# Decays of a chunked state-space scan: fp32r products of 32 rows and a mask product in place of triangles spread by GpSimd

## The chip, the core and the metric

The kernel runs on one core of a Trainium2 chip. A core has five engines that run side by side: TensorE (PE in the profile; its weight loads are the row PEld), VectorE (DVE), ScalarE (ACT), GpSimd (POOL) and SyncE (SP), which here only issues DMAs. The metric is device time in microseconds (us), as the median of several runs; lower is better.

## The reference, cut to what matters

The model is a block of dense layers (gated convolution, attention, cross attention, MLP), then a second block: a mixer that holds a Mamba-2 scan (SSD), and a product-key expert layer. The change is in the scan. With 256 tokens and 16 meta tokens the scan has three chunks of 128 positions (the first one only its last 16), 24 heads of 64 in 4 groups of 6 heads, and a state of 128:

```
a = dt * A                                   # per position and head
a_cs = cumsum(a)                             # inside a chunk
decay_in = exp(segsum(a))                    # segsum[i, j] = a_cs[i] - a_cs[j] for i >= j, else -inf
cb = einsum('bclgn,bcsgn->bgcls', Cc, Bc)
y_diag = einsum('bgcls,bgrcls,bcsgrp->bclgrp', cb, decay_in, x_dt)
```

For each of the 24 heads and two chunks a 128x128 matrix of decays is needed: the exponential of a difference of running sums, and zero above the diagonal. The rest of the scan (states of the chunks, their decay, the output from the state) is not changed.

## The kernel before

Products of the dense layers are made in fp32r pairs: each 512 KB block of weights is fetched by SP into one of four slots (`raw`), cast by ACT to its high part `wh`, and DVE subtracts to get the low part `wl`; PE then takes three products for each piece (`wh` by high and low rows, `wl` by high rows). A block may be fetched into a slot when the block four before it has been split, and cast when PE has used the one four before it. All engines follow an order written out by hand, with semaphores between them, so the sequence on each engine is that of the code.

Stages around the change, in order: the MLP of the first block; `post(2)` and `norm(4)` (residual and RMS norm, where PE has nothing else to do than keep its clock up); the `xbc` blocks in five groups of four, of which PE makes a product of 272 tokens each, ACT copies it from the bank `AO` to `XB`, and DVE runs a convolution of 16 instructions a group (`conv4`) and splits the next blocks; in between, `dtz` (the steps dt and the decays a) is made by DVE and ACT, and five small products of `dtz` with the triangles `upper`, `later` and `ones` give the running sums, of which ACT makes `exs`; then the `z` blocks with transposes; then the scan.

The scan is a loop of 16 steps k on PE, ACT and DVE: step k is three heads of a group (two steps a group, 8 steps a chunk). On PE step k is: `seg(k+1)`, which makes the three 128x128 matrices of differences of the next step in `AO`; the products of step k with `XDT` into `Y` (they wait for `seg_m`); a product with the state (`from_state`) in even steps, `second_state` in odd steps of the first chunk; and in nine steps the 24 products of an `sc` block (`sc_wide`), which is dense work of the next part laid in between. ACT takes the exponential of `AO` (`EE`), DVE multiplies it with the masked correlations `CBM` (`MM`). Before the change `seg` is

```
mm(AO[:, 0, 0:3 * P], later[:, :], AU[:, k % 2, :, :], True, True)
```

in plain f32, where `AU` (128 x 3 x 128) is the triangle `upper` times a head's decays, made on GpSimd by `decay_inputs(k)`, two steps ahead of PE. GpSimd also adds the skip term and multiplies with the gate for four pieces of the output (`skip_and_gate`), the places of three of them being set by `SKIP_AT`.

Of the kernel before, what the change touches and what calls it, by code (L numbers as in the profile page):

```python
# [23 lines left out]
P = 128  # L24
# [8 lines left out]
D = 1024  # L33
# [79 lines left out]
SKIP_AT = {7: (0, 0), 10: (0, 1), 11: (0, 2)}  # L113
# [3 lines left out]
WARM_UP, KEEP_WARM = 32, 32  # L117

# [22 lines left out]
def build(nc, stream, gain_cols, cols, rows, post_gains, x, mem, meta, keys_in, out, h2_spill):  # L141
    ctx = ExitStack()
    with ctx:
# [18 lines left out]
        ident = sb("ident", [P, P])  # L162
# [7 lines left out]
        stat = sb("stat", [P, 48])  # L170
        choice_at = (nc.sbuf_base + 31) // 32 * 32
# [6 lines left out]
        def at(name, shape, offset, dt=F32, base=None):  # L178
# [49 lines left out]
        AU = at("AU", [P, 2, 3, P], 124192)  # L228
# [65 lines left out]
        meta_ss, meta_rstd, meta_scaled = sem("meta_ss"), sem("meta_rstd"), sem("meta_scaled")  # L294
# [4 lines left out]
        v_out, f_prod, mv_out = sem("v_out"), sem("f_prod"), sem("mv_out")  # L299
# [19 lines left out]
        au_done, seg_prod, seg_exp, seg_m, y_prod = (sem(n) for n in (  # L319
            "au_done", "seg_prod", "seg_exp", "seg_m", "y_prod"))  # L320
# [8 lines left out]
        numbered, hot, g_prod, g_out = sem("numbered"), sem("hot"), sem("g_prod"), sem("g_out")  # L329
        hot2, ranked, curve, up_part = sem("hot2"), sem("ranked"), sem("curve"), sem("up_part")  # L330
# [98 lines left out]
        def _(sp):  # L429
# [49 lines left out]
        def _(act):  # L479
# [60 lines left out]
            def meta_square():  # L540
                nc.scalar.activation(xn[0:META, 2, :], metax[:, :], ACT.Square,
                                     accum_out=stat[0:META, 2:3]).then_inc(meta_ss, 1)
# [104 lines left out]
            for s in range(8):  # L647
# [4 lines left out]
                if s == 7:  # L652
                    values_high(s - 2)
                    act.wait_ge(w_used, LAST["mv"])
                    nc.scalar.copy(MV[:, :, :], Y[:, 1, :].rearrange("p (j c) -> p j c", j=TT)).then_inc(mv_out, 1)
# [114 lines left out]
            mlp("mlp", FF_CHUNKS, mlp_hid, mlp_act, mlp_ah, 0)  # L770
            meta_high()
# [31 lines left out]
            nc.scalar.activation(exs[0:META, 96:120], M[0:META, 1, 96:120], ACT.Exp).then_inc(ac_exp, 1)  # L803
            xbc_groups(3, XBC_T // 4)
# [241 lines left out]
        def _(dve):  # L1046
# [49 lines left out]
            def meta_scale():  # L1096
                dve.wait_ge(meta_rstd, 1)
# [20 lines left out]
            nc.vector.memset(UP[:, :, 0:CONV_W - 1], 0.0).then_inc(conv_pad, 1)  # L1118
            dve.wait_ge(gain_in, 16)
# [271 lines left out]
            for r, o, n in parts:  # L1391
# [4 lines left out]
                    .then_inc(dt_a, 1)  # L1396

# [29 lines left out]
            nc.vector.tensor_tensor(exs[:, 48:72], exs[:, 48:72], dtz[:, 2, 24:48], ALU.mult).then_inc(xdd_w, 1)  # L1427
            xbc_groups(3, XBC_T // 4)
# [253 lines left out]
            dve.wait_ge(ranked, 1)  # L1682
# [33 lines left out]
            dve.wait_ge(numbered, 1)  # L1716
# [100 lines left out]
        def _(pool):  # L1817
# [6 lines left out]
            nc.gpsimd.affine_select(out=ident[:, :], in_=ident[:, :], pattern=[[-1, P]], compare_op=ALU.not_equal,  # L1824
# [35 lines left out]
            for p in range(3):  # L1860
                post(p)
                norm(2 + p)
                if p == 0:
                    pool.wait_ge(meta_ss, 1)
                    inverse_root(stat[0:META, 10:11], stat[0:META, 2:3], D, meta_rstd)
# [35 lines left out]

# [729 lines left out]
```

## Time and profile before

| | |
|---|---|
| median of 3 runs | 1449.78 us (1449.65 to 1450.62) |
| profiled execution | 1451.42 us, of which the span of the trace is 1449.7 us |
| busy in the span | PE 1419.8 us (98%), PEld 1255.3, DVE 1082.9 (75%), ACT 793.9 (55%), POOL 71.5 (5%) |
| granted TensorE clock | 0.996 of full speed |
| chain that ended last | PE 87%, DVE 8%, ACT 3%, issue 1%, POOL 1% |

The span is the time from the first to the last instruction of one execution. Busy times of engines overlap, so they don't add up to it. The chain is followed back from the last instruction, at each step to what released it; only work on it can lengthen or shorten the run directly.

### The profile page before, as it was taken

The page shows a single profiled execution, that of the slowest core. Times are in us where ns is not written, and L with a number is a line of the kernel's source. Part 1 is how long each engine was busy: PE and PEld are TensorE (multiplying, and loading weights), DVE is VectorE, ACT ScalarE, POOL GpSimd, SP SyncE. Part 2 cuts the span into 40 slices and gives each one's busy share as a digit, 9 for nine tenths or more (in the row PEclk, how much of TensorE's full clock was granted, in tenths as well). Part 3 has the DMA queues.
Part 4 walks back from the last instruction along what each step waited for, and adds up shares of the span by engine and source line. Part 5 has one row for each costly group of instructions (what it writes and reads, how often), then busy time and mean ns, then how long its engine had stood idle before and what let it go on. Part 6 is the DMA issues. An engine that isn't in the chain of part 4 may idle for free.

```text
span 1449.7 us, 25954 instructions
## 1 busy us (share of the span) xinstructions
PE 1419.8 (98%) x8633; PEld 1255.3 (87%) x8633; DVE 1082.9 (75%) x2053; ACT 793.9 (55%) x1307; POOL 71.5 (5%) x68
## 2 busy tenths in 40 slices
PE   8999999999999999999999999999999999999998
PEld 8977878888898887799999999888888888788886
DVE  6997776666688588599999997566666666667776
ACT  6755764545576435455555445455555555545444
POOL 0000000000001562000000000000000000000000
PEclk9999999999999999999999999999999999999999
DMA  7523335655345423554656887657557575667753
GB/s 291 193 102 117 130 126 185 196 188 188 131 146 178 144 85 115 182 182 146 204 186 223 253 257 258 217 186 248 190 187 252 186 256 188 198 223 248 252 196 145
DMA packets 103354, 274.57 MB, mean 189 GB/s; under 512 B 8176, under 2 KB 41072, under 8 KB 102784
## 3 DMA queue, kind: packets, MB, share of 16 engines
q1 hardware_dynamic: 64832, 237.11, 49.2%
q10 hardware_dynamic: 38176, 34.63, 7.3%
q0 software_dynamic: 288, 2.10, 0.5%
q8 instruction: 32, 0.52, 0.1%
q14 instruction: 26, 0.21, 0.0%
HBM read 254.93 MB, written 18.87 MB: 189 GB/s over the span
## 4 chain that ended last, share of the span: by engine, by line
PE 87%; DVE 8%; ACT 3%; issue 1%; POOL 1%; DVEq 0%; ACTq 0%; POOLq 0%
PE Y L1954 44%; PE AO L1954 39%; PE M L1954 2%; DVE wl L1054 2%; ACT wh L490 1%; DVE I L1603 1%; DVE SCO L1619 1%; DVE I L1617 1%; ACT xhl L533 0%; PE M L2044 0%; DVE X L1270 0%; DVE V L1625 0%; DVE V L1611 0%; DVE xn L1267 0%; PE M L2318 0%
## 5 line engine op out<-in xcount | busy, mean ns | idle before, releaser
L1054 DVE TENSOR_TENSOR wl<-raw,wh 128x1024 fp32r<-128x1024 f32 x440 | 545.2, 1243 | 199.8 <-ACT wh L490 199.3
L1954 PE MATMUL AO<-xhl,wh 128*128 128x256 f32 (+3 forms) x2784 | 649.7, 316 | 5.3 <-DVE wl L1054 2.5
L490 ACT CAST wh<-raw 128x1024 fp32r<-128x1024 f32 x440 | 461.0, 1050 | 142.4 <-PE Y L1954 75.7
L1954 PEld LDWEIGHTS AO<-xhl,wh 128*128 128x128 f32 x2784 | 456.2, 189 | 38.0 <-issue 2.8
L1954 PE MATMUL AO<-xhl,wl 128*128 128x256 f32 (+2 forms) x1776 | 485.2, 282 | 0.0
L1954 PEld LDWEIGHTS AO<-xhl,wl 128*128 128x128 f32 x1776 | 334.4, 188 | 7.9
L1954 PE MATMUL Y<-wh,peer_ah 128*128 128x512 f32 x512 | 199.9, 390 | 3.1 <-DVE peer_al L1751 3.1
L1954 PE MATMUL Y<-wh,peer_al 128*128 128x512 f32 x512 | 200.0, 391 | 0.0
L1954 PE MATMUL Y<-wl,peer_ah 128*128 128x512 f32 x512 | 199.9, 390 | 0.0
L972 ACT CAST peer_ah<-hid 128x256 fp32r (+1 forms) x128 | 52.0, 406 | 182.7 <-DVE hid L1745 95.9
L1954 PEld LDWEIGHTS Y<-wh,peer_ah 128*128 128x128 f32 x512 | 96.6, 189 | 21.5 <-DVE peer_al L1751 2.3
L1954 PEld LDWEIGHTS Y<-wl,peer_ah 128*128 128x128 f32 x512 | 96.4, 188 | 20.4
L1954 PEld LDWEIGHTS Y<-wh,peer_al 128*128 128x128 f32 x512 | 96.5, 188 | 20.0
L1751 DVE TENSOR_TENSOR peer_al<-hid,peer_ah 128x256 fp32r<-128x256 f32 x128 | 54.4, 425 | 73.7 <-ACT peer_ah L972 73.7
L913 ACT ACTIVATE hid<-AO 128x256 f32<-128x256 f32 (+1 forms) x64 | 24.6, 384 | 90.4 <-PE AO L1954 90.3
L1728 DVE TENSOR_SCALAR hots<-numbers,picks 128x128 f32<-128x128 f32 x256 | 68.4, 341 | 0.0
L1843 POOL TENSOR_SCALAR stat<-stat 128x1 f32<-128x1 f32 x12 | 6.6, 547 | 1152.3 <-ACT fin_j L1032 822.4
L1954 PE MATMUL Y<-hots 128*128 128x128 f32 x512 | 62.4, 275 | 0.0
L1954 PEld LDWEIGHTS Y<-hots 128*128 128x128 f32 x512 | 59.9, 192 | 0.0
L1745 DVE TENSOR_TENSOR hid<-hid,gates (+1 forms) x128 | 53.4, 418 | 2.1 <-issue 0.6
L1954 PE MATMUL Y<-wh,mlp_ah 128*128 128x512 f32 x128 | 50.1, 391 | 1.2 <-DVE mlp_al L1339 1.2
L1149 DVE SCALAR_TENSOR_TENSOR CV<-UP,colp,CV 128x256 f32<-128x256 f32 x120 | 50.3, 476 | 0.3 <-ACT CV L578 0.3
(330 smaller groups left out, 1623.8 us busy)
## 6 DMA issues: line engine op xcount, KB each, us to landing
raw<-in_stream SPq DMA_DIRECT2D x440, 512.0 KB, 3.3
gate_spill<-gstage ACTq DMA_DIRECT2D x32, 512.0 KB, 5.0
gates<-gate_spill ACTq DMA_DIRECT2D x6, 2048.0 KB, 15.1
gates<-gate_spill ACTq DMA_DIRECT2D x8, 512.0 KB, 6.9
rowg<-in_post SPq DMA_DIRECT2D x3, 512.0 KB, 4.3
X<-in_x SPq DMA_DIRECT2D x2, 512.0 KB, 4.8
memx<-in_mem SPq DMA_DIRECT2D x1, 1024.0 KB, 7.6
keys<-in_keys POOLq DMA_DIRECT2D x1, 1024.0 KB, 7.1
```

What stands on the lines that cost most here:

```text
L490: nc.scalar.copy(wh[:, s, :], raw[:, s, :]).then_inc(split_hi, 1)
L913: nc.scalar.activation(hid[:, c, :], AO[:, s % 2, 0:T], ACT.Gelu).then_inc(a_free, 1)
L972: nc.scalar.copy(peer_ah[:, s, :], hid[:, slot, :]).then_inc(hid_hi, 1)
L1054: nc.vector.tensor_tensor(wl[:, s, :], raw[:, s, :], wh[:, s, :].bitcast(F32), ALU.subtract)\
L1149: nc.vector.scalar_tensor_tensor(out=CV[:, c, :], in0=src, scalar=col("conv_w", c * CONV_W + w), in1=CV[:, c, :], op0=ALU.mult, op1=ALU.ad ...
L1603: step(nc.vector.max_index(pos[:, 8:16], top[:, 8:16], vals))
L1617: step(nc.vector.max_index(pos[:, 0:8], top[:, 0:8], vals))
L1619: swapped = step(nc.vector.match_replace(vals, top[:, 0:8], vals, 3 * NEG))
L1728: ins = nc.vector.tensor_scalar(hots[:, s, 1, t, :], numbers[:, :], picks[:, 0, k:k + 1], picks[:, 2, k:k + 1], ALU.is_equal, ALU.mult)
L1745: nc.vector.tensor_tensor(h, h, gates[:, w % 2, :, bass.ds(k * BATCH, BATCH)], ALU.mult)\
L1751: nc.vector.tensor_tensor(peer_al[:, s, :], hid[:, slot, :], peer_ah[:, s, :].bitcast(F32), ALU.subtract).then_inc(hid_lo, 1)
L1954: return nc.tensor.matmul(o, a, b, start=start, stop=stop)
```

## The change

`seg(k)` gets two fp32r products instead of one f32 product. The first has only 32 rows in the contraction: the stationary operand `RS` has, for each group of 6 heads, a strip of 32 partitions with the running sums of the heads as rows (high part and low part, each 6 rows) and two rows of ones for each chunk; the moving operand `RV` has in the same strip a pattern that picks the head, and in the rows beside the ones the running sums of the other position. Their product is the difference of the sums. The second product adds, through the identity, a 128x128 mask `RM` (0 on and below the diagonal, -2^100 above it), read three times by a stride of zero.

What feeds them is new: at the start three small DVE instructions make `row_pick` from the identity; GpSimd makes `RM`, clears `RA` and sets its ones after the third norm; ACT fills `RV` with 128 x 768 elements behind the MLP; DVE copies the decays twice into `RA`; PE makes two more f32 products with `upper`; ACT copies them (`RH`), DVE makes high and low part (`RS`), and SP carries rows of `RS` into `RV` by 16 DMAs of 6 x 128 elements, placed ahead of the third fetch of a `z` block. `decay_inputs` and `AU` are gone from GpSimd. Some semaphores are merged, which leaves their waits where they were.

```
+            act.wait_ge(picked, 3)
+            act.wait_ge(meta_scaled, 1)
+            act.wait_ge(at_pv, len(groups))
+            nc.scalar.activation(RV[:, :, :], row_pick[:, LO_ROW + FOX_H:LO_ROW + FOX_H + HG][:, :, None]
+                                 .to_broadcast([P, HG, P]), ACT.Copy).then_inc(picked, 1)
             meta_high()
             post(2)
...
             nc.scalar.activation(exs[0:META, 96:120], M[0:META, 1, 96:120], ACT.Exp).then_inc(ac_exp, 1)
+            nc.scalar.copy(RH[:, :, :], M[:, 1, P:3 * P].rearrange("p (c l) -> p c l", c=2)).then_inc(line_hi, 1)
             xbc_groups(3, XBC_T // 4)
...
+            dve.wait_ge(dt_a, 2)
+            dve.wait_ge(line_cols, 3)
+            for r in (0, LO_ROW):
+                nc.vector.tensor_copy(
+                    RA[:, :, :].rearrange("p c (g r) -> p c g r", r=ROWS_OF)[:, :, :, r:r + HG],
+                    dtz[:, 3, 24:72].rearrange("p (c g r) -> p c g r", c=2, g=SSD_G)).then_inc(line_cols, 1)
...
+            dve.wait_ge(line_hi, 1)
+            nc.vector.scalar_tensor_tensor(out=RS[:, :, :], in0=RH[:, :, :].bitcast(F32),
+                                           scalar=row_pick[:, LO_ROW + 2 * FOX_H:],
+                                           in1=M[:, 1, P:3 * P].rearrange("p (c l) -> p c l", c=2),
+                                           op0=ALU.mult, op1=ALU.subtract).then_inc(line_lo, 1)
             xbc_groups(3, XBC_T // 4)
...
+            def lines():
+                sp.wait_ge(picked, 4)
+                sp.wait_ge(line_lo, 1)
+                for g in range(SSD_G):
+                    for c in range(2):
+                        for n, r in ((0, 0), (1, LO_ROW)):
+                            o, f = ROWS_OF * g + ONE_ROW + 2 * c + n, ROWS_OF * g + r
+                            sp.dma_start(RV[o:o + 1, :, :].bitcast(F32), RS[f:f + HG, c, :].bitcast(F32)).then_inc(lines_in, 16)
...
             for n in range(24):
                 b = STREAM["z"] + n
+                if n == 2:
+                    lines()
                 sp.wait_ge(split_lo, b - 3)
...
-            mm(M[0:META, 1, 96:120], later[0:META, 0:META], a0, True, True).then_inc(ac_prod, 1)
+            mm(M[0:META, 1, 96:120], later[0:META, 0:META], a0, True, True)
+            pe.wait_ge(line_cols, 5)
+            for c in range(2):
+                ins = mm(M[:, 1, P * (c + 1):P * (c + 2)], RA[:, c, :], upper[:, :], True, True)
+            ins.then_inc(ac_prod, 1)
             xbc_groups(3, XBC_T // 4)
...
             def seg(k):
-                pe.wait_ge(au_done, k + 1)
+                c, s = divmod(k, 8)
                 if k:
                     pe.wait_ge(seg_exp, k)
-                mm(AO[:, 0, 0:3 * P], later[:, :], AU[:, k % 2, :, :].rearrange("p a b -> p (a b)"),
-                   True, True).then_inc(seg_prod, 1)
+                else:
+                    pe.wait_ge(lines_in, 16 * 4 * SSD_G)
+                    pe.wait_ge(consts, 10)
+                r = slice(ROWS_OF * (s // 2), ROWS_OF * (s // 2) + ROWS_OF)
+                h = slice(3 * (s % 2), 3 * (s % 2) + 3)
+                mm(AO[:, 0, 0:3 * P], RS[r, c, :], RV[r, h, :].rearrange("p a b -> p (a b)"), True, False)
+                mm(AO[:, 0, 0:3 * P].rearrange("p (a b) -> p a b", a=3), ident_r[:, :],
+                   RM[:, None, :].to_broadcast([P, 3, P]), False, True).then_inc(seg_prod, 1)
...
-            for k in range(2, 16):
-                decay_inputs(k)
-                if k in SKIP_AT:
-                    skip_and_gate(*SKIP_AT[k])
+            for p in range(3):
+                skip_and_gate(0, p)
```

On PE, at steps 1 and 2 of the scan, the rows before are these (the row with AU is `seg`; an f32 product counts here as one instruction, and as two in the trace):

```order
L1954 MATMUL AO<-AU,later 128x384 [waits seg_exp,au_done]
L1954 MATMUL Y<-XDT,MM 128x64 [waits seg_m]
L1954 MATMUL Y<-XDT,MM 128x64 x2
L1954 MATMUL M<-XDD,BN 128x384 [waits xdd_done]
L1954 MATMUL AO<-AU,later 128x384 [waits seg_exp,au_done]
```

With the change the same place reads:

```order
L1999 MATMUL AO<-RV,RS 128x384 [waits seg_exp]
L1999 MATMUL AO<-RM,ident 128x384
L1999 MATMUL Y<-XDT,MM 128x64 [waits seg_m]
L1999 MATMUL Y<-XDT,MM 128x64 x2
L1999 MATMUL M<-XDD,BN 128x384 [waits xdd_done]
L1999 MATMUL AO<-RV,RS 128x384 [waits seg_exp]
L1999 MATMUL AO<-RM,ident 128x384
```

A product of 32 rows stands now between two of 128 rows, in each of the 16 steps, and the wait for GpSimd (`au_done`) is gone.

On POOL, from the middle of the scan to the first group norm, before (YO_92 and YO_93 are the outputs of the two chunks):

```order
L1882 TENSOR_TENSOR AU<-dtz,upper 128x384 [waits seg_prod] x3
L1921 TENSOR_TENSOR YO_92<-YO_92,XT 128x512 [waits xd_done,y_add]
L1924 TENSOR_TENSOR YO_92<-YO_92,Z 128x512 [waits z_out,pool_step]
L1882 TENSOR_TENSOR AU<-dtz,upper 128x384 [waits seg_prod]
L1921 TENSOR_TENSOR YO_92<-YO_92,XT 128x512 [waits xd_done,y_add]
L1924 TENSOR_TENSOR YO_92<-YO_92,Z 128x512 [waits z_out,pool_step]
L1882 TENSOR_TENSOR AU<-dtz,upper 128x384 [waits seg_prod] x4
L1837 TENSOR_SCALAR stat<-stat 128x4 [waits grp_ss]
```

And with the change:

```order
L1968 TENSOR_TENSOR YO_92<-YO_92,XT 128x512 [waits xd_done,y_add]
L1971 TENSOR_TENSOR YO_92<-YO_92,Z 128x512 [waits z_out,pool_step]
L1968 TENSOR_TENSOR YO_92<-YO_92,XT 128x512 [waits xd_done,y_add]
L1971 TENSOR_TENSOR YO_92<-YO_92,Z 128x512 [waits z_out,pool_step]
L1883 TENSOR_SCALAR stat<-stat 128x4 [waits grp_ss]
```

The second and third piece follow each other directly; no triangles stand between them or behind them.

On ACT, at the end of the MLP, before:

```order
L747 CAST mlp_ah<-mlp_act 128x256 [waits hid_prod]
L547 ACTIVATE xhl<-M,gain 128x16 [waits meta_turned]
L547 ACTIVATE xhl<-M,gain 128x16 x7
L552 ACTIVATE eps<-eps 128x1
L686 ACTIVATE junk,stat<-Y 128x512 [waits first_rows]
```

And with the change:

```order
L768 CAST mlp_ah<-mlp_act 128x256 [waits hid_prod]
L795 ACTIVATE RV<-row_pick 128x768 [waits at_pv,meta_scaled,picked]
L568 ACTIVATE xhl<-M,gain 128x16 [waits meta_turned]
L568 ACTIVATE xhl<-M,gain 128x16 x7
L573 ACTIVATE eps<-eps 128x1
L707 ACTIVATE junk,stat<-Y 128x512 [waits first_rows]
```

The fill of `RV` stands ahead of the eight instructions (`meta_high`) that write the high part of the meta tokens' rows.

## Rows read from the trace of the kernel before

**Rows 1.** Busy time of each engine in one stretch, the scan: length, then engines

```profile
498.40:562.00 63.60, 61.68 (x413) 52.41 (x412) 51.06 (x76) 24.75 (x49) 30.07 (x24) 1.00 0.25 84
```

**Rows 2.** Timeline of PE at step 0: start, duration, engine, line, operation, tile

```profile
502.46 0.81 PE L1954 MATMUL AO<-AU,later 128*128 128x384 f32 x2
503.10 0.78 PE L1954 MATMUL Y<-XDT,MM 128*128 128x64 f32 x6
```

**Rows 3.** Timeline of PE around the first products of 16 rows

```profile
491.57 0.28 PE L1954 MATMUL AO<-xhl,wl 128*128 128x258 f32 x1
491.78 1.55 PE L1954 MATMUL M<-XDM,BN 16*128 16x384 f32 x4
493.26 0.51 PE L1954 MATMUL Y<-xhl,wh 128*128 128x258 f32 x2
493.61 0.28 PE L1954 MATMUL Y<-xhl,wl 128*128 128x258 f32 x1
```

**Rows 4.** Timeline of PE around the transposes of the meta rows

```profile
369.22 0.39 PE L1954 MATMUL AO<-xhl,wh 128*128 128x512 f32 x1
369.54 0.67 PE L2061 MATMUL M<-ident,xn 16*128 16x16 f32 x8
...
370.47 0.40 PE L1954 MATMUL Y<-wl,mlp_ah 128*128 128x512 f32 x1
370.70 0.40 PE L1954 MATMUL Y<-wh,mlp_al 128*128 128x512 f32 x1
```

**Rows 5.** Timelines of ACT and DVE behind the MLP

```profile
370.97 0.41 ACT L747 CAST mlp_ah<-mlp_act 128x256 fp32r<-128x256 f32 x1
371.28 1.42 ACT L547 ACTIVATE xhl<-M,gain 128x16 fp32r<-128x16 f32 x8
...
372.88 1.22 DVE L1104 SCALAR_TENSOR_TENSOR xhl<-M,gain,xhl 128x16 fp32r<-128x16 f32 x8
...
385.31 2.04 ACT L490 CAST wh<-raw 128x1024 fp32r<-128x1024 f32 x2
```

**Rows 6.** Timelines of DVE and PE at the decays and the group behind

```profile
404.70 0.29 DVE L1387 SCALAR_TENSOR_TENSOR dtz<-dtz 16x24 f32<-16x24 f32 x2 [2.20 <-ACT dtz L789]
405.02 0.29 DVE L1392 SCALAR_TENSOR_TENSOR dtz<-dtz,rowp 16x24 f32<-16x24 f32 x2
...
412.86 0.51 PE L1954 MATMUL AO<-xhl,wh 128*128 128x272 f32 x2 [0.15 <-DVE wl L1054]
```

**Rows 7.** Timelines of ACT and PE behind the exponentials of the running sums

```profile
432.00 0.39 ACT L559 COPY XB<-AO 128x272 f32 x1
...
432.05 0.29 PE L1954 MATMUL AO<-xhl,wl 128*128 128x272 f32 x1
432.44 0.52 PE L1954 MATMUL AO<-xhl,wh 128*128 128x272 f32 x2
```

**Rows 8.** Timelines of POOL, DVE and PE at step 10

```profile
536.46 1.14 POOL L1882 TENSOR_TENSOR AU<-dtz,upper 128x384 f32<-128x384 f32 x1
...
539.89 1.28 POOL L1924 TENSOR_TENSOR YO<-YO,Z 128x512 f32<-128x512 f32 x1
540.17 1.42 DVE L1535 TENSOR_TENSOR MM<-EE,CBM 128x384 f32<-128x384 f32 x1 [1.49 <-ACT EE L842]
541.64 0.88 PE L1954 MATMUL Y<-XDT,MM 128*128 128x64 f32 x6 [0.47 <-DVE MM L1535]
```

**Rows 9.** Timeline of DVE at steps 8 and 14

```profile
532.57 0.55 DVE L1535 TENSOR_TENSOR MM<-EE,CBM 128x384 f32<-128x384 f32 x1
...
553.83 1.68 DVE L1535 TENSOR_TENSOR MM<-EE,CBM 128x384 f32<-128x384 f32 x1 [1.77 <-ACT EE L842]
```

**Rows 10.** Timelines of DVE and ACT at block fetches; last the DMA issues

```profile
434.29 2.34 DVE L1054 TENSOR_TENSOR wl<-raw,wh 128x1024 fp32r<-128x1024 f32 x2
...
448.20 1.06 ACT L490 CAST wh<-raw 128x1024 fp32r<-128x1024 f32 x1
...
raw<-in_stream SPq DMA_DIRECT2D x440, 512.0 KB, 3.3
```

More of the change, by code:

```diff
@@ L117 @@
 WARM_UP, KEEP_WARM = 32, 32
+ROWS_OF = 32
+MASKED = 2.0 ** 100
+ONE_ROW, LO_ROW = 6, 10
 def turned_tiles():
@@ L227, in build @@
         CBM = at("CBM", [P, 4, P], 98336)
-        AU = at("AU", [P, 2, 3, P], 124192)
+        RV = at("RV", [P, HG, P], 124192, F32R)
+        RS = at("RS", [P, 2, P], 26208, F32R)
+        RA = at("RA", [P, 2, P], 27232)
+        RH = at("RH", [P, 2, P], 78048, F32R)
+        RM = at("RM", [P, P], 130336, F32R)
         EE = at("EE", [P, 2, 3, P], 127264)
@@ L318, in build @@
         st_prod, st_done = sem("st_prod"), sem("st_done")
-        au_done, seg_prod, seg_exp, seg_m, y_prod = (sem(n) for n in (
-            "au_done", "seg_prod", "seg_exp", "seg_m", "y_prod"))
+        picked, line_cols, line_hi, line_lo, lines_in = (sem(n) for n in (
+            "picked", "line_cols", "line_hi", "line_lo", "lines_in"))
+        seg_prod, seg_exp, seg_m, y_prod = (sem(n) for n in (
+            "seg_prod", "seg_exp", "seg_m", "y_prod"))
         off_prod, off_done = sem("off_prod"), sem("off_done")
@@ L654, in _ @@
                     act.wait_ge(w_used, LAST["mv"])
-                    nc.scalar.copy(MV[:, :, :], Y[:, 1, :].rearrange("p (j c) -> p j c", j=TT)).then_inc(mv_out, 1)
+                    nc.scalar.copy(MV[:, :, :], Y[:, 1, :].rearrange("p (j c) -> p j c", j=TT)).then_inc(v_out, 1)
                     act.wait_ge(dec_done, 3 * FOX_H)
@@ L1118, in _ @@
             nc.vector.memset(UP[:, :, 0:CONV_W - 1], 0.0).then_inc(conv_pad, 1)
+            dve.wait_ge(consts, 5)
+            at_row = row_pick[:, 0:LO_ROW + FOX_H]
+            nc.vector.tensor_reduce(at_row, ident[:, :].rearrange("p (g r) -> p r g", r=ROWS_OF)[:, 0:LO_ROW + FOX_H, :],
+                                    AX_X, ALU.add).then_inc(picked, 1)
+            dve.wait_ge(picked, 1)
+            nc.vector.tensor_reduce(row_pick[:, LO_ROW + 2 * FOX_H:], at_row[:, LO_ROW:], AX_X, ALU.add)\
+                .then_inc(picked, 1)
+            nc.vector.tensor_tensor(row_pick[:, LO_ROW + FOX_H:LO_ROW + 2 * FOX_H], at_row[:, 0:FOX_H],
+                                    at_row[:, LO_ROW:], ALU.add).then_inc(picked, 1)
             dve.wait_ge(gain_in, 16)
@@ L1823, in _ @@
             pool.wait_ge(consts, 4)
-            nc.gpsimd.affine_select(out=ident[:, :], in_=ident[:, :], pattern=[[-1, P]], compare_op=ALU.not_equal,
+            nc.gpsimd.affine_select(out=ident_r[:, :], in_=ident[:, :], pattern=[[-1, P]], compare_op=ALU.not_equal,
                                     fill=1.0, base=0, channel_multiplier=1).then_inc(consts, 1)
@@ L1900, in group_norm @@
                 inverse_root(stat[:, 28:32], stat[:, 24:28], GW, grp_rstd)
+            nc.gpsimd.memset(RM[:, :].bitcast(F32), 0.0).then_inc(consts, 1)
+            pool.wait_ge(consts, 9)
+            nc.gpsimd.affine_select(out=RM[:, :], in_=RM[:, :].bitcast(F32), pattern=[[1, P]], compare_op=ALU.is_ge,
+                                    fill=-MASKED, base=0, channel_multiplier=-1).then_inc(consts, 1)
+            nc.gpsimd.memset(RA[:, :, :], 0.0).then_inc(line_cols, 1)
+            pool.wait_ge(line_cols, 1)
+            for c in range(2):
+                o = ONE_ROW + 2 * c
+                nc.gpsimd.memset(RA[0:1, c, :].rearrange("p (g r) -> p g r", r=ROWS_OF)[:, :, o:o + 2], 1.0)\
+                    .then_inc(line_cols, 1)
             pool.wait_ge(xdd_w, 2)
@@ L2303, in _ @@
             mm(M[:, 1, 72:96], ones[:, :], a1, True, True)
-            mm(M[0:META, 1, 96:120], later[0:META, 0:META], a0, True, True).then_inc(ac_prod, 1)
+            mm(M[0:META, 1, 96:120], later[0:META, 0:META], a0, True, True)
+            pe.wait_ge(line_cols, 5)
+            for c in range(2):
+                ins = mm(M[:, 1, P * (c + 1):P * (c + 2)], RA[:, c, :], upper[:, :], True, True)
+            ins.then_inc(ac_prod, 1)
             xbc_groups(3, XBC_T // 4)
```

40 lines of the change are left out of this document (16 added, 24 removed).

## The prediction, made before the changed kernel ran

> **What bounds the kernel now.** I read the busy shares first, then the chain that ended last, then the timeline of the stretch that is changed. In the scan PE is busy for 61.68 of 63.60 us, DVE for 51.06 and GpSimd for 30.07 [rows 1]. So a product taken from PE is worth its length there, unless PE stands at a wait anyway, and GpSimd matters only through those whom it holds up. The chain passes on PE through the `seg` products of 13 of the 16 steps. The other three (2, 11 and 15) lie in front of a wait for DVE's `MM` and are worth nothing. Outside of the scan the change adds work at three places where PE waits for ACT or DVE; there the reader has to look at who is late, not at PE's share.
>
> **The segments on PE.** Before, the two passes of a `seg` start at 502.46 and the next product at 503.10: 0.64 us [rows 2]. The new products are fp32r. Two products of 512 columns in this type start 0.23 us apart [rows 4], so 384 columns take 0.17 and two of them 0.35. By this alone a segment saves 0.29 us and the 13 on the chain 3.8.
>
> But the first of the two has 32 rows and stands between products of 128. The trace has such a change with 16 rows and the same 384 columns: from 491.57, the start of the last full product, to 493.61, the start of the third one behind the four narrow passes, is 2.04 us [rows 3]. The work in it is one product of 258 columns (0.12, scaled from 0.23 for 512), four f32 passes at 0.32, and two of 258 columns (0.24): 1.65. So going to the narrow tile and back costs 0.39 us. It shows at two points: the narrow pass starts 0.21 behind the full one, not 0.12, and the first full product behind takes 0.35 with its weights, not 0.24 for two. The second witness is smaller: eight transposes of 16 rows between 369.22 and 370.47 [rows 4]. Take off 0.23 for the product before, 0.23 for the one behind, and 0.53 for eight starts (0.67 less the 0.21 of a tail, over seven, times eight), and 0.26 is left. I take 0.39, since that row has the same width. A new segment then costs 0.35 + 0.39 = 0.74, 0.10 more than the old one, and 13 of them +1.3 us. With 0.26 it would be 0.61, and -0.4 in all.
>
> The Trainium skill says the same as a rule: a change of tiling mode, and not merely of the tile, drains TensorE (TensorEngine Tiling (Array Packing), Key Properties). It gives no figure; without the rule the segments would be worth -3.8, with the rows' price +1.3, and the trace of before agrees with the rule.
>
> **What GpSimd lets go.** `MM` reads two operands from SBUF and takes 0.55 us undisturbed [rows 9]. At step 10 it takes 1.42, since GpSimd is inside the gate of the third piece (539.89 to 541.17), and PE waits for it [rows 8]. Without the triangle of 1.14 us that GpSimd makes between the second and the third piece [rows 8], the gate ends near 540.0, before `MM` starts at 540.17. `MM` then ends 0.87 earlier. PE gets at most 0.6 of that, as the products in front of 541.64 end at about 541.0. I count -0.6; it is 0 if GpSimd's third piece is late by 0.2. At step 14 `MM` takes 1.68 [rows 9], but GpSimd works there on the fourth piece, which stands where it stood, so nothing is gained. The wait of PE for `MM` at step 1 hangs on a chain through ACT's cast and DVE's taps and not on GpSimd. The other triangles lie beside splits that nobody waits for.
>
> The Trainium skill has the mechanism: the pair of SBUF ports that DVE shares with GpSimd is an exclusive lock, kept for a whole instruction by whoever starts first, and a DVE instruction with two SBUF inputs needs it (SBUF — State Buffer, SBUF: two separate sides). The 1.42 and 1.68 in place of 0.55 agree.
>
> **Behind the MLP.** ACT's fill of `RV` stands ahead of `meta_high`. A cast of 1024 elements keeps ACT for 1.0 us (2.04 for two) and one of 256 for 0.31 (370.97 to 371.28), so 768 cost about 0.77 [rows 5]. `meta_high` ends at 372.70 now, and DVE starts its low part at 372.88. Both move: 371.28 + 0.77 + 1.42 = 373.47, so DVE starts at about 373.5, 0.6 later. DVE is on the chain from there (it weighs the rows of Y next, for which ACT waits, and PE does nothing but keep its clock until the norm is there). +0.6 us; 0.4 if the broadcast source is quick, 0.8 if it is slow.
>
> **At the decays.** DVE's two copies into `RA` wait for `dt_a`, which the two instructions before them set. A pair of such small instructions with the wait behind it takes 0.32 (404.70 to 405.02) [rows 6]. Behind them stands `conv4`, and then the split for which PE waits before 412.86 [rows 6]. +0.3 us, up to 0.5 with the strided rows.
>
> **At the running sums.** PE makes two more f32 products of 128 columns (four passes, about 0.45 us) and ACT casts 256 columns of them, 0.3 us as above [rows 5]. ACT's copy at 432.00 is what PE waits for: its last product started at 432.05 and ends at about 432.2, and the next starts at 432.44 [rows 7]. ACT moves that start to 432.75, and PE's own addition only to about 432.65, so it is covered: +0.3 us. DVE's new instruction of 256 columns (0.45) comes before splits, of which the third waited 0.6 for ACT; nothing.
>
> **On SP.** The 16 small DMAs stand ahead of the third fetch of `z`. They can start when DVE is through with the pair of splits that ends at 436.6 [rows 10]. The block behind them lands 3.3 us after its issue, and its cast stands at 448.20 and will stand about 1.2 later by the terms above [rows 10]. So the 16 issues have 449.4 - 3.3 - 436.6 = 9.5 us, 0.6 for one. What the issue of so small a DMA takes no row shows. Up to 0.6 us it costs nothing, and I take that; beyond, ACT's cast and copies are late, and from about 0.8 on PE is, since its own use of the block comes one block of 3 us later. The three instructions on DVE at the start run while it waits for x, and GpSimd's new ones in a pause: nothing.
>
> **The sum.** +1.3 (segments) - 0.6 (GpSimd) + 0.6 (`RV`) + 0.3 (`RA`) + 0.3 (`RH`) = +1.9 us. The profiled execution took 1451.42 with a span of 1449.7, and would take 1453.3; the median of the runs, 1449.78, is 1.6 below that execution, and I carry the difference over: 1451.7 us, or 0.13% more. This kernel's measurement tells about 0.2%, or 2.9 us, from no change.
>
> **The rivals.**
> 1. The forecast: narrow products cost the switch of 0.26 to 0.39. Segments -0.4 to +1.3, the rest 0.2 to 1.6: 1449.6 to 1452.7. Chance 0.60.
> 2. Only a part of the switch is paid, because weights of a 32-row strip are loaded ahead (a third to a half of 0.39). A segment costs 0.5, 13 give -1.8; with the rest +0.6 it is 1448.6. For it: the long weight load in the row of 16 rows was of the f32 type. Against it: both witnesses show the loss on the return too, where the weights are full ones. Chance 0.12.
> 3. The switch is free in fp32r: -3.8 + 0.6 = -3.2, and `MM` of step 14 then starts before GpSimd's gate, which gives up to 0.9 more: 1446.6 to 1445.7, faster. For it: both witnesses are f32. Against it: the product behind, which was late as well, was fp32r. Chance 0.15.
> 4. Slower: the mask product reads its moving operand with a stride of zero, and the narrow one a strip of 32 partitions, and no row shows either; if both go at the pace of an f32 pass (0.32), a segment costs 0.64 + 0.39 = 1.03, 13 give +5.1, and with +0.6 it is 1455.5. It decides from 0.82 us a segment on (2.3 us over 13 on top of the 0.6). One alone gives 0.89, +3.3, 1453.7. Chance 0.10.
> 5. The DMAs on SP take over 0.8 us each, and the `z` blocks come late by some us: over 1453. Chance 0.03.
>
> **How the numbers follow.** The time is that of case 1. Cases 3 to 5 lie on both ends; the range 1445.9 to 1453.5 takes in case 1 with its bounds, case 2 and most of case 3, and leaves out 4 and 5 and the end of 3. The likeliest case's own range is 1449.6 to 1452.7. Faster by over 0.2%: 0.16 (case 3 and a little of 2). Slower by over 0.2%: 0.15 (cases 4, 5 and a little of 1). Within: 0.69.
>
> **What the profile after would show.** From the start of the last `sc` product before a segment to that of the `Y` product behind it there should be 0.12 + 0.74 us; 0.12 + 0.35 means case 3, over 0.95 case 4. `MM` of step 10 should take 0.55, with no wait of PE for it. DVE's low meta rows should start 0.6 later than now against the last MLP product, the split behind `conv4` 0.3 later against the copy of `dtz`, and PE's wait behind 432 should be 0.3 of ACT's work longer, less its own two products. SP's 16 issues should take under 9.5 us and the third `z` cast wait for no DMA. The prediction is wrong if the price of the narrow tile isn't that of the 16 rows, or if a wait of PE shows in the scan that isn't there now.

## The result, and the profile after

The changed kernel takes 1454.03 us (median of 6 runs, 1452.01 to 1455.51); the kernel before took 1450.2 beside it (6 runs). The ratio is 1.0025, with a 95% interval of 1.0015 to 1.0035: slower by 0.25%, 2.3 us above the forecast and above the end of the range. The profiled execution took 1452.03 us, with a span of 1450.3 and a granted clock of 0.999.

Runs of one kernel differ by more than the terms looked for here, and most of the difference goes with the granted clock. Over the 167 runs that list their clock, a kernel's time falls by 0.86 us for each 0.001 of clock (one slope fitted to all of them, with a level of its own for each kernel; 0.54 us of scatter are left). So beside each median stands the level: the time that the fit gives for this kernel at a clock of 0.999. A level is good to about 0.2 us. For the kernel before it is 1448.3 (68 runs), for the changed one 1452.4: 4.0 us apart.

The page after, busy times and chain:

```profile
PE 1419.1 (98%) x8637; PEld 1252.6 (86%) x8637; DVE 1078.9 (74%) x2059; ACT 794.3 (55%) x1309; POOL 58.0 (4%) x57
...
PE 84%; DVE 9%; ACT 3%; issue 1%; SPq 1%; DMA 1%; POOL 0%; DVEq 0%; ACTq 0%
```

DVE and GpSimd have less to do, but the chain now passes for 1% each through SP's queue and through a DMA. The same stretch as in [rows 1]:

```profile
498.40:562.00 63.60, 62.85 (x410) 52.59 (x409) 46.02 (x74) 24.70 (x47) 14.24 (x11) 1.00 0.25 84
```

PE stands still for 0.75 us of it and not for 1.9. So the scan isn't where the time went. I paired the 440 `wl` splits of DVE in the two traces, one by one, and took the difference of their starts, below called the offset: how much later the changed kernel is at this point. By stage it grows or falls so (us):

| stretch | grows by | forecast |
|---|---|---|
| MLP of the first block (213.6 to 371.8 before) | +2.07 | 0 |
| meta rows and norm (to 386.4) | +0.73 | +0.6 |
| decays (400.8 to 411.5) | +0.31 | +0.3 |
| running sums (426.7 to 437.2) | +0.27 | +0.3 |
| `z` blocks (448.8 to 477) | +0.66 | 0 |
| scan (498.4 to 571) | -0.19 | +0.7 |
| `wout2` (573 to 617) | -0.73 | 0 |

The largest entry is a stage in which the change touches no instruction.

**The MLP.** Its products with the low rows, first those of the kernel before, then those after (one form's 128 products: shortest, median and longest, first and last start):

```profile
L1954 PE MATMUL Y<-wh,mlp_al x128: 389/389/398, 204.5 to 375.9; 128*128 128x512 f32 x128
```

```profile
L1999 PE MATMUL Y<-wh,mlp_al x128: 389/393/404, 204.4 to 378.1; 128*128 128x512 f32 x128
```

From first to last it is 171.4 us before and 173.7 after. The timeline shows where: in a row of products without any wait. Before and after:

```profile
210.92 0.39 PE L1954 MATMUL Y<-wh,mlp_ah 128*128 128x512 f32 x1
211.15 0.39 PE L1954 MATMUL Y<-wl,mlp_ah 128*128 128x512 f32 x1
211.37 0.39 PE L1954 MATMUL Y<-wh,mlp_al 128*128 128x512 f32 x1
211.60 0.39 PE L1954 MATMUL Y<-wh,mlp_ah 128*128 128x512 f32 x1
```

```profile
210.91 0.40 PE L1999 MATMUL Y<-wh,mlp_ah 128*128 128x512 f32 x1
211.14 0.40 PE L1999 MATMUL Y<-wl,mlp_ah 128*128 128x512 f32 x1
211.38 0.40 PE L1999 MATMUL Y<-wh,mlp_al 128*128 128x512 f32 x1
211.61 0.39 PE L1999 MATMUL Y<-wh,mlp_ah 128*128 128x512 f32 x1
```

Three products take 0.68 us before and 0.70 after; over the 384 the median distance of two starts is 227 ns before and 231 to 232 after. With `mixh` and `mixl` (96 products) it goes from 227 to 232 too; with `m2h` and `m2l` (192) the other way, from 233 to between 226 and 232. The table leaves out one more such piece, `wout` (126 to 160 us), where it grows by 0.4. What these products have in common is that their stationary operands lie in the arena, which the new tile `row_pick` (108 bytes per partition, rounded up) moves up by 128 bytes. The arena is the large tile of on-chip memory (SBUF) in which most other tiles of the kernel have a fixed offset. Products whose stationary operand lies elsewhere keep their pace (227 ns with `peer_ah`, before and after).

**A segment.** PE after, at steps 0 and 2; the rows answer to [rows 2]:

```profile
506.43 0.28 PE L1999 MATMUL AO<-xhl,wl 128*128 128x258 f32 x1
506.63 0.43 PE L1999 MATMUL AO<-RV,RS 32*128 32x384 f32 x1
...
513.17 0.86 PE L1999 MATMUL M<-XDD,BN 128*128 128x384 f32 x2
513.97 0.43 PE L1999 MATMUL AO<-RV,RS 32*128 32x384 f32 x1
514.33 0.44 PE L1999 MATMUL AO<-RM,ident 128*128 128x384 f32 x1
514.61 0.55 PE L1999 MATMUL Y<-XDT,MM 128*128 128x64 f32 x4
```

The narrow product and the mask product start 0.36 apart, and the next one 0.28 behind the mask product: 0.64, and close to 0.10 more is lost ahead of the narrow one (it starts 0.20 to 0.21 behind a product that otherwise takes 0.12). That is the 0.74 of the forecast.

**MM at step 10**, answering to [rows 8]:

```profile
542.89 2.13 POOL L1971 TENSOR_TENSOR YO<-YO,Z 128x512 f32<-128x512 f32 x1
544.35 0.78 PE L1999 MATMUL Y<-XDT,MM 128*128 128x64 f32 x6
545.08 0.56 DVE L1582 TENSOR_TENSOR MM<-EE,CBM 128x384 f32<-128x384 f32 x1 [1.18 <-ACT EE L869]
545.75 0.82 PE L1999 MATMUL Y<-XDT,MM 128*128 128x64 f32 x6
```

The gate ends at 545.02, 0.06 before `MM` starts, and PE's wait for it is gone, as forecast. The margin is thin: in e4 and e8 below, in which PE reaches this point sooner, the gate lies across `MM` again, `MM` takes 1.14 and 1.17, and PE waits 0.56 and 0.58 for it.

**SP, and ACT behind it:**

```profile
438.97 1.47 SPq L491 DMA_DIRECT2D raw<-in_stream  x2
440.55 12.08 SPq L483 DMA_DIRECT2D RV<-RS  x16
452.68 51.31 SPq L491 DMA_DIRECT2D raw<-in_stream  x20
```

```profile
451.24 0.39 ACT L580 COPY XB<-AO 128x272 f32 x1 [1.40 <-PE AO L1999]
456.32 1.05 ACT L511 CAST wh<-raw 128x1024 fp32r<-128x1024 f32 x1 [4.70 <-DMA raw<-in_stream]
```

Sixteen issues take 12.08 us, 0.755 for one (most start 0.72 apart). The forecast gave them 9.5 us of room; the rows give 7.4. The cast would have started at 451.6 without its wait of 4.70, it starts 3.6 behind the issue of its block, and the sixteen start at 440.55: 451.6 - 3.6 - 440.55.

**ACT's fill of `RV`** took 0.84 us:

```profile
373.06 0.41 ACT L768 CAST mlp_ah<-mlp_act 128x256 fp32r<-128x256 f32 x1
373.37 0.84 ACT L795 ACTIVATE RV<-row_pick 128x768 fp32r<-128x768 f32 x1
374.11 1.42 ACT L568 ACTIVATE xhl<-M,gain 128x16 fp32r<-128x16 f32 x8
```

My theory A: the pace of a product hangs on the address of its stationary operand modulo 256 bytes, and that, with SP's DMAs, is what the forecast lacked. The main rival (B below): something new in the kernel, or the run, disturbs the MLP.

### The profile page after: what moved, and what is told of

It reads as the page before. It is cut to its first block, busy times and chain, and to the rows that moved or that the text cites. A ratio compares the mean times of both kernels' runs of the same rounds, so it can differ in the third digit from the quotient of the medians.

```text
span 1450.3 us, 25966 instructions
## 1 busy us (share of the span) xinstructions
PE 1419.1 (98%) x8637; PEld 1252.6 (86%) x8637; DVE 1078.9 (74%) x2059; ACT 794.3 (55%) x1309; POOL 58.0 (4%) x57
## 4 chain that ended last, share of the span: by engine, by line
PE 84%; DVE 9%; ACT 3%; issue 1%; SPq 1%; DMA 1%; POOL 0%; DVEq 0%; ACTq 0%
PE Y L1999 44%; PE AO L1999 37%; DVE wl L1081 3%; PE M L1999 2%; ACT wh L511 1%; SPq L483 1%; DVE XS L1453 1%; DVE I L1650 1%; DVE SCO L1666 1%; DVE I L1664 1%; DVE X L1306 0%; DVE V L1672 0%; DVE V L1658 0%; DVE xn L1303 0%; DVE xhl L1113 0%
## 5 line engine op out<-in xcount | busy, mean ns | idle before, releaser
L1999 PE MATMUL Y<-wl,mlp_ah 128*128 128x512 f32 x128 | 50.5, 395 | 0.0
```

Source lines behind the costliest of these rows:

```text
L1999: return nc.tensor.matmul(o, a, b, start=start, stop=stop)
```

## The experiments

Eleven kernels ran. "Ratio" is against the kernel before, with its 95% interval; "level" is the time at a clock of 0.999 (error 0.2 us, 0.3 for e2, e8 and e9).

| run | median, us | ratio | level, us |
|---|---|---|---|
| changed kernel | 1454.03 | 1.0025 (1.0015 to 1.0035) | 1452.4 |
| e1_shift | 1451.88 | 1.0011 (1.0002 to 1.0020) | 1450.4 |
| e10_by_64 | 1453.41 | 1.0026 (1.0016 to 1.0037) | 1451.5 |
| e11_by_256 | 1450.18 | 1.0002 (0.9993 to 1.0011) | 1448.6 |
| e7_place | 1447.90 | 0.9987 (0.9978 to 0.9996) | 1447.6 |
| e2_unshift | 1454.21 | 1.0037 (1.0023 to 1.0051) | 1450.8 |
| e3_spread | 1452.70 | 1.0022 (1.0013 to 1.0032) | 1451.6 |
| e5_fill_later | 1453.75 | 1.0025 (1.0014 to 1.0037) | 1451.7 |
| e6_pool_ra | 1453.41 | 1.0028 (1.0018 to 1.0038) | 1451.9 |
| e9_decoy | 1458.44 | 1.0052 (1.0036 to 1.0069) | 1454.1 |
| e4_full_rows | 1449.35 | 0.9997 (0.9988 to 1.0006) | 1447.9 |
| e8_all | 1442.98 | 0.9960 (0.9947 to 0.9974) | 1443.2 |

### Where the tiles lie: e1, e10, e11, e7, e2

e1, on the kernel before:

```
         stat = sb("stat", [P, 48])
+        pad = sb("pad", [P, 27])
```

> The kernel before, with nothing but an unused tile of 108 bytes per partition (the size of row_pick) allocated at its place, which moves the arena and every tile in it up by 128 bytes. Theory A (the 2.0 us that the MLP lost and the 0.4 of wout come from where the stationary operands mlp_ah, mlp_al, mixh and mixl lie): the products of Y with mlp_ah and mlp_al start 231 to 232 ns apart and not 227, those with mixh and mixl too, those with m2h and m2l 226 to 232 and not 233, and the time is 1.2 to 2.0 us above the kernel before (0.08 to 0.14%). Rival B (an effect of the new instructions or of the run, and not of the addresses): products at 227 ns, time as before within 0.4 us.

The MLP's first and last product with `mlp_al` are 173.7 us apart, as after the change, the distances are 231 to 232 ns, and the kernel is 2.1 us slower by level (1.2 to 2.0 expected). One unused tile, and no instruction changed. Rival B is out.

e10 is the same with `[P, 16]`, e11 with `[P, 64]`.

> The kernel before with an unused tile of 64 bytes per partition, so that the whole arena lies 64 bytes higher. By theory A the address modulo 256 sets the pace: mlp_ah, mlp_al, mixh and mixl lie at 192, where m2h lay, and their 480 products go from 227 to about 233 ns (+2.9 us); m2h and m2l lie at 0, where mlp_ah lay in the changed kernel, and theirs go from 233 to 231 or 232 (-0.3 us): +2.6 us. Rival O (only multiples of 128 bytes count, or the pace hangs on the tile and not on its address): mlp at 227, time as before.

> The kernel before with an unused tile of 256 bytes per partition. By theory A with a period of 256 bytes nothing changes: mlp and mix at 227 ns, m2h and m2l at 233 to 234, time within 0.3 us of before. Rival P (the period is longer, or any move of the arena costs): at least one of the two groups changes its pace.

The groups by form of e1, e10 and e11 (busy time and mean duration of one, in ns, behind the bar):

```profile
L1955 PE MATMUL Y<-wl,mlp_ah 128*128 128x512 f32 x128 | 50.5, 395 | 0.0
```

```profile
L1955 PE MATMUL Y<-wh,mlp_al 128*128 128x512 f32 x128 | 50.5, 395 | 0.0
```

```profile
L1955 PE MATMUL Y<-wl,mlp_ah 128*128 128x512 f32 x128 | 49.8, 389 | 0.0
```

In e10 the 480 products of `mlp` and `mix` start 233 to 234 ns apart and those of `m2h` and `m2l` 231 to 232; the level rises by 3.2 us (2.6 expected). In e11 all are as before (227; 233 to 236), and the level by 0.3. So the period divides 256 bytes, and 64 or 128 bytes is not one. Rivals O and P are out.

e7, on the kernel before:

```
-        Z = at("Z", [P, TT, D_SSD], 28288)
-        m2h = at("m2h", [P, 16, T], 40576, F32R)
-        m2l = at("m2l", [P, 16, T], 56960, F32R)
+        Z = at("Z", [P, TT, D_SSD], 28224)
+        m2h = at("m2h", [P, 16, T], 40512, F32R)
+        m2l = at("m2l", [P, 16, T], 56896, F32R)
```

and `XDT`, `XDD`, `XDM` and the first `YO` by 64 bytes as well.

> The kernel before, with m2h and m2l (the stationary operands of wout2) 64 bytes lower, and their neighbours Z, XDT, XDD, XDM and the first YO too, so that their addresses modulo 256 become those of mlp_ah in the kernel before; no instruction is changed. Theory A (the address of the stationary operand modulo 256 bytes sets the pace of such products: 227 ns at 128, 231 to 232 at 0, 233 to 234 at 192): the 192 products of Y with m2h and m2l go from 233 to 227 ns and the time falls by 1.0 to 1.3 us. Rival K (the pace hangs on something else of the stage, such as the DMA's share there): still 233 ns, no change.

All three forms go to 226 to 227 ns; before and in e7:

```profile
L1954 PE MATMUL Y<-wl,m2h 128*128 128x512 f32 x64 | 25.2, 394 | 0.0
```

```profile
L1954 PE MATMUL Y<-wl,m2h 128*128 128x512 f32 x64 | 24.9, 389 | 0.0
```

From the first of these splits to the last the offset falls by 1.1 us, and the level is 0.7 below the kernel before (1.0 to 1.3 expected): faster, with nothing but addresses changed. Rival K is out.

e2, on the changed kernel, has the tile behind the arena:

```
-        row_pick = sb("row_pick", [P, LO_ROW + 2 * FOX_H + 1])
...
         arena = sb("arena", [P, 32 * BLK])
+        row_pick = sb("row_pick", [P, LO_ROW + 2 * FOX_H + 1])
```

> The changed kernel with row_pick allocated behind the arena, so that all older tiles lie where they lay before the change. Theory A: the MLP products are back at 227 ns, m2h and m2l at 233, the MLP loses nothing against the kernel before, and the time is 1.2 to 2.0 us below the changed kernel, about 0.14% above the kernel before. Rival B: spacing and time stay those of the changed kernel.

The trace does what theory A says: 227 ns in the MLP, 233 for `m2h`, and 171.4 us from the first to the last product with `mlp_al`. The median does not: 1454.21, no less than the changed kernel, where 1.2 to 2.0 us less had been expected, so by its time alone this run speaks for rival B. Its five runs were granted clocks of 0.993 to 0.996, the six of the changed kernel 0.995 to 0.999. By level it is 1.5 us faster (error 0.4), and at the one clock that both had, 0.995, its two runs took 1454.2 and that of the changed kernel 1455.5. This correction was made after the result was seen. Why this kernel was granted less clock is open; e8, with the same addresses and more, was granted 0.998 on average.

### SP: e3

```
             for n in range(24):
                 b = STREAM["z"] + n
-                if n == 2:
-                    lines()
+                if 2 <= n < 10:
+                    lines(n - 2)
```

where `lines(n)` issues the two DMAs of one group and chunk.

> The changed kernel with SP's 16 small DMAs no longer in one piece ahead of the third z fetch, but two ahead of each of eight fetches (the third to the tenth). Theory C (16 issues of 0.72 us hold the fetch up by 12 us, and PE pays about 0.7 us for the block that is late): two issues take 1.5 us and every block lands before its cast; ACT's waits of 4.7 and 1.1 us for a DMA are gone, the offset against the kernel before rises by nothing in the z stage, and the time is 0.6 to 0.8 us below the changed kernel. Rival D (the loss there comes from PE's two extra products, ACT's cast of RH and DVE's RS, not from SP): ACT's waits go and the time stays within 0.2 us.

SP and ACT in the same place:

```profile
440.71 1.60 SPq L483 DMA_DIRECT2D RV<-RS  x2
442.36 0.43 SPq L491 DMA_DIRECT2D raw<-in_stream  x1
```

```profile
451.39 0.39 ACT L580 COPY XB<-AO 128x272 f32 x1 [1.41 <-PE AO L1999]
451.67 1.06 ACT L511 CAST wh<-raw 128x1024 fp32r<-128x1024 f32 x1
```

The issues cost what they cost before, and the cast waits for nothing. The offset grows by 0.07 in the `z` stage, not by 0.66, and the level is 0.7 lower. Theory C holds. The 0.66 is that of one execution: in the five other kernels that keep the sixteen in one piece (e2, e4, e5, e6, e9) the offset grows there by 0.5 to 1.1.

### ACT and DVE ahead of the scan: e5 and e6

e5 puts the five lines of the fill behind `thin_copy` of the first `xbc` group; e6 gives the loop over `RA` to GpSimd, with the same waits.

> The changed kernel with ACT's fill of RV no longer ahead of meta_high but behind ACT's second copy of the xbc stage (the copy of thin_t), where ACT waits 2.6 us for PE. Theory G (the fill of 0.84 us on ACT moves the whole norm, in which PE has nothing to do, by its length less an overlap of 0.1 to 0.2): the low meta rows of DVE start 0.7 us earlier against the last MLP product, and the time is 0.6 to 0.8 us below the changed kernel. Rival H (the norm waits for DVE's residual sum or for PE's last MLP products anyway): no change within 0.2 us.

> The changed kernel with the two copies of the decays into RA made by GpSimd in place of DVE. Theory I (the pair with its wait costs DVE 0.3 us in a stretch where PE waits for DVE's splits): 0.2 to 0.3 us less. Rival J (the copies on GpSimd and the taps of DVE get into each other's way, since both read SBUF): no gain, or up to 0.3 us more. A difference of this size is at the edge of what the times can tell; the offset of DVE's splits behind the convolution in the trace decides.

In e5 the norm follows the MLP 0.6 us closer (the offset grows by 0.13 there, not by 0.73), since ACT goes on at once:

```profile
374.10 0.41 ACT L768 CAST mlp_ah<-mlp_act 128x256 fp32r<-128x256 f32 x1
374.41 1.42 ACT L568 ACTIVATE xhl<-M,gain 128x16 fp32r<-128x16 f32 x8
```

In e6 the offset doesn't grow at the decays, where it grew by 0.31. GpSimd needs 0.69 us for the pair, and DVE's first taps beside it take 1.40 as they did:

```profile
408.78 0.69 POOL L1947 COPY RA<-dtz 128x48 f32<-128x48 f32 x2 [23.26 <-DVE dtz L1428]
```

```profile
408.64 1.40 DVE L1444 TENSOR_SCALAR XS<-XB,colp 128x272 f32<-128x272 f32 x4
```

The levels fall by 0.6 and 0.5, with an error of 0.3 for such a difference (by medians it is only 0.3 and 0.6). Rivals H and J are out by the traces, not by the times.

### The scan: e4 and e9

e4, on the changed kernel, takes the first product over 128 rows. GpSimd writes each group's strip of `RS` into an operand of its own with zeros elsewhere:

```
+            for k in range(8):
+                c, g = divmod(k, SSD_G)
+                r = slice(ROWS_OF * g, ROWS_OF * g + ROWS_OF)
+                pool.wait_ge(consts, 12 + k)
+                nc.gpsimd.tensor_copy(padded[k][r, :], RS[r, c, :].bitcast(F32)).then_inc(consts, 1)
...
-                mm(AO[:, 0, 0:3 * P], RS[r, c, :], RV[r, h, :].rearrange("p a b -> p (a b)"), True, False)
+                mm(AO[:, 0, 0:3 * P], padded[4 * c + s // 2], RV[:, h, :].rearrange("p a b -> p (a b)"), True, False)
```

> The changed kernel with the first product of a segment over 128 rows in place of 32: eight stationary operands, each with one group's strip of RS and zeros in the other strips (made by GpSimd with two clears and eight copies of 32x128 before the scan, in tiles that are free there); the result is the same. Theory E (going to the 32-row tile and back costs 0.39 us a segment, as forecast): a segment costs 0.35 in place of 0.74, 13 of them on the chain give 5.1 us less, less what DVE's MM then makes PE wait in the scan, which I put at 1 to 2 us: 3 to 5 us below the changed kernel, and 0.5 to 1.5 us below the kernel before. Rival F (the 0.74 is the pace of the two new products, by the stride of zero of the mask or by the shape, and not the change of tile): a segment stays above 0.6 us and the time falls by less than 1.5.

```profile
508.10 0.28 PE L2012 MATMUL AO<-xhl,wl 128*128 128x258 f32 x1
508.22 0.33 PE L2012 MATMUL AO<-RV,RZ 128*128 128x384 f32 x1
508.39 0.34 PE L2012 MATMUL AO<-RM,ident 128*128 128x384 f32 x1
508.56 0.78 PE L2012 MATMUL Y<-XDT,MM 128*128 128x64 f32 x6
```

A segment takes 0.34 here and 0.34 to 0.36 in the other steps with such neighbours, and the loss ahead of it is gone. The mask product, with its stride of zero, takes 0.17, the pace of any other. Everything between 0.35 and 0.74 is the narrow tile. The offset falls by 4.6 us in the scan (0.2 with the 32 rows) and the level by 4.5. Theory E holds and rival F is out.

e9, on the changed kernel, brings GpSimd's triangles back, for nobody:

```
+            for k in range(2, 16):
+                decoy(k)
+                if k in (7, 10, 11):
+                    skip_and_gate(0, (7, 10, 11).index(k))
```

where `decoy` is `decay_inputs` with its waits, and a spare tile as output.

> The changed kernel with GpSimd's old triangles put back in their old places and behind their old waits, but written into a spare tile that nobody reads. Theory M (what the scan gained beside PE's segments comes from GpSimd's triangles alone, which lay in front of gates and so stretched DVE's MM): MM of step 10 takes 1.4 us again, PE waits for it, and the scan gets back what it gained there in steps 10, 12 and 14 (0.79, 0.17 and 0.24 us): +0.8 to +1.2 us against the changed kernel. Rival N (the gain comes from the new segments, whose AO is ready earlier, so that EE and MM start earlier): the scan and the time stay within 0.3 us.

```profile
545.32 1.28 POOL L1983 TENSOR_TENSOR YO<-YO,Z 128x512 f32<-128x512 f32 x1
545.73 1.28 DVE L1583 TENSOR_TENSOR MM<-EE,CBM 128x384 f32<-128x384 f32 x1 [1.63 <-ACT EE L870]
546.55 2.91 POOL L1929 TENSOR_TENSOR spare<-dtz,upper 128x384 f32<-128x384 f32 x2
547.07 1.24 PE L2013 MATMUL Y<-XDT,MM 128*128 128x64 f32 x6 [0.51 <-DVE MM L1583]
```

The gate lies beside `MM` again, `MM` takes 1.28 us, and PE waits. The time rises more than theory M said (0.8 to 1.2), by 1.7 us by level and 4.4 by median. The two of its six runs that were granted 0.999 took 1453.3 and 1453.45, which is 1.3 to 1.4 above the two of the changed kernel at 0.999. The windows tell the rest in part (the last columns are the granted clock, the DMA share and GB/s):

```profile
540.00:545.00 5.00, 5.00 (x35) 4.42 (x35) 4.10 (x5) 1.80 (x3) 4.92 (x3) 1.00 0.30 105
545.00:550.00 5.00, 4.50 (x20) 3.34 (x20) 4.24 (x4) 1.88 (x3) 4.31 (x4) 0.74 0.37 114
550.00:555.00 5.00, 5.00 (x33) 4.39 (x32) 2.60 (x6) 1.46 (x3) 0.83 (x1) 0.92 0.28 99
```

Behind the wait the mean clock of a window falls to 0.74 and 0.92, which is a stretch at 1.2 in place of 2.4 GHz: 0.26 and 0.08 of 5 us are 1.7 us of full-speed work lost. The wait alone doesn't explain it: the kernel before has the same wait (0.47 at 541.64) and a longer one of 0.73 at step 14, and its clock stays at 1.00 from 540 to 565. The offset against the changed kernel rises by 2.66 over the scan (0.71 to 3.37); without that 1.7 it is 0.96, inside the 0.8 to 1.2. Theory M holds in its mechanism, and rival N is out; the price in time is 1.3 to 1.7 and not 0.8 to 1.2, and why e9 is granted less clock (0.993 to 0.995 in four of six runs) is open.

### All of it: e8

> All of it on the changed kernel: row_pick behind the arena, SP's 16 DMAs two by two, segments over 128 rows, the fill of RV later, RA by GpSimd, and m2h, m2l and their neighbours 64 bytes lower. If the terms are independent they add: about -1.5 (or -2.0 by the spacing alone), -0.7, -4.5, -0.7, -0.3 and -1.2 against the changed kernel, or -8.9 us: 1445.1, which is 4.9 us or 0.34% below the kernel before. Rival L (they don't add, since DVE's MM or the blocks of weights take the place of what is taken away, or since a PE with less waits is granted less clock): between 1446 and 1449.

1442.98 us, 0.40% faster than the kernel before and 11 us faster than the changed one. By level it is 9.1 below the changed kernel, where the expected terms add up to 8.9 and the levels measured one by one to 8.6. They are independent as far as this can tell, and rival L is out: in the scan PE's weight loads wait 2.3 us for `MM` in all, in four places, against 1.3 in the changed kernel.

## Why the prediction was wrong

The forecast was 1451.7 for the median and +1.9 us of difference; the difference is +3.8 by medians and +4.0 by level (the other 0.4 of the 2.3 is that the kernel before took 1450.2 beside it and not 1449.78). Two steps failed: the sum had no term for where the tiles lie, which cost 1.8 us, and it put SP's sixteen DMAs at nothing, which cost 0.7. Neither of the two signs by which the prediction was to be known wrong came true: the narrow tile has the price of the 16 rows, and the scan has no wait of PE that wasn't there. The steps one by one:

- **The segments on PE** (+1.3 for 0.74 against 0.64): right in the price, a little high in the count. The rows show 0.74, and e4 shows that 0.39 to 0.40 of it is the narrow tile. By the starts of the `Y` products it comes to about 1.0 in all: 0.2 up to step 0, 0.06 to 0.10 for each of steps 2 to 9, and only 0.02 to 0.04 at steps 11, 13 and 15. The Trainium skill's rule that a change of tiling mode drains TensorE (TensorEngine Tiling (Array Packing), Key Properties) agrees with that: 0.74 with the narrow tile, 0.34 without. The 16-row f32 passes of [rows 3] gave the right price for a 32-row fp32r product.
- **What GpSimd lets go** (-0.6): right in the mechanism, too small. From the `Y` products of step 9 to those of step 10 PE takes 1.40 us where it took 2.19. That is 0.8 in place of the 0.6 at most that I allowed. Step 12, where a triangle of GpSimd stretched `MM` to 0.77, gave 0.17, and step 14 0.24 (`MM` at 1.43 in place of 1.68); both I had put at nothing. The scan came out at -0.2 and not +0.7, which hid 0.9 us of what failed elsewhere. The shared port that the Trainium skill describes (SBUF — State Buffer, SBUF: two separate sides) agrees with `MM` at 0.56 without and 1.28 with GpSimd's gate beside it.
- **Behind the MLP** (+0.6): +0.73, from a fill of 0.84 and not 0.77. e5 takes 0.6 of it away. **At the decays** (+0.3): +0.31. **At the running sums** (+0.3): +0.27.
- **On SP** ("Up to 0.6 us it costs nothing, and I take that"): this step failed, in both of its numbers. An issue took 0.755 us on average, not 0.6. And the room was 7.4 us, not 9.5: I had moved the cast by the 1.2 of the other terms, but left the start of the sixteen at 436.6, while the splits that they wait for move as well, and the issue of the second fetch stands before them (start at 440.55, cast due at 451.6). With 7.4 of room and the same 3 us, my own rule has PE late from 0.65 us an issue on, not from 0.8. The cast as first victim and PE after it were right. It cost 0.66, and e3 takes it away. Rival 5 had the mechanism and too high a threshold.
- **What no step had**: this is the larger failure, a term put at nothing without a reason. The forecast went through every instruction that the diff touches, and not through the allocation ahead of them. `row_pick` stands in the diff as one line of memory and moves the whole arena. It cost 0.4 us in `wout` (96 products, 4 to 5 ns each), 2.1 in the MLP (384 products, 5 to 6 ns) and gave back 0.7 in `wout2`: +1.8 us. e1 reproduces it without the rest of the change (+2.1 by level), and e2 takes it away (-1.5 by level).

Together: +1.9 forecast, +1.8 for the addresses, +0.7 for SP, -0.9 for the scan, +0.1 for the fill is 3.6, against 3.8 to 4.0. Up to 0.4 us stays unassigned, within the error of the levels (0.2 each). The missing term weighs most: without it the time would have been about 1452.2, well inside the range. Without SP's 0.7 alone it would have been 1453.3, just inside; and had the scan cost the +0.7 of the forecast, it would have been about 1454.9.

## What to carry to other kernels

Read a diff's allocations as closely as its instructions: when a kernel is bound by PE, list the address modulo 256 of each stationary operand before and after, and count its products. A product over a few rows between full ones costs 0.39 us here and saves PE nothing, since its 384 columns stay; padding the operand with zeros, by an engine that is idle, was worth 4.5 us. Price a batch of small DMA issues by its number and deal it out between the fetches that share the queue. When a term moves the end of a time window, move its start too.

## What the runs showed of the hardware

- The distance of two fp32r products of 512 columns depended on the address of the 128x128 stationary operand modulo 256 bytes: 226 to 227 ns at 128, 231 to 232 at 0, 233 to 236 at 192, 226 to 232 at 64 (medians over 32 to 128 products each, in ten kernels). The moving operands `wh` and `wl` lay at 128 in all of them. The moving operand's address seems to count as well: products of 256 columns that stream `mh` or `ml`, with `wh` or `wl` stationary, had medians of 117 to 118 ns before (`mh` and `ml` at 96) and 119 to 121 after (at 224), over 32 products each; no experiment was made on this. So whether the stationary operand's address sets the pace alone, or its distance from the moving one's, is open, and no run tells why.
- SP mostly took 0.72 to 0.76 us from start to start of two small DMAs (6 x 128 elements, from SBUF to SBUF), whether 16 or 2 came together; the first took 0.91. Behind them, the fetches of 512 KB started 0.47 apart.
- `MM` beside a gate of GpSimd: in all seven cases in which the gate had started first, `MM` ended 0.41 to 0.42 us behind the gate's end, and so took 1.14 to 1.68 in place of 0.55 (steps 10 and 14 before and in e9, step 14 in the changed kernel, step 10 in e4 and e8). Where `MM` had started 0.05 us before the gate (step 14 in e4 and e8), `MM` took 0.56, and the gate 1.64 to 1.65 in place of 1.28.
- Stretches at half clock come and go between kernels. The profiled execution of the kernel before has two that the one after lacks. One of them, before:

```profile
610.00:612.00 2.00, 1.05 (x8) 0.86 (x8) 1.09 (x5) 1.02 (x3) 1.24 (x3) 1.00 0.71 66
612.00:614.00 2.00, 1.56 (x10) 1.45 (x9) 1.46 (x4) 1.15 (x4) 0.00 (x0) 0.67 0.83 295
614.00:616.00 2.00, 2.00 (x11) 2.00 (x10) 2.00 (x6) 2.00 (x7) 0.00 (x0) 0.50 0.94 262
```

It follows a stretch in which PE was busy for 1.05 of 2 us. The changed kernel pauses in the same place (busy for 1.92 of 4 us, 612 to 616), and its clock stays at 1.00. The stretch in e9 follows a wait of 0.51. The clock accounts for 80% of the variance between the runs of one kernel, and without it beside each time e2 would have been read as a failure of the theory.
